# A hybrid decoder step: a new order for the seven-product MLP chunks, and one weight split per chunk on GpSimd

## The chip, the cores and the metric

One NeuronCore of one Trainium2 chip. The metric is the device time of one launch in microseconds (us). TensorE multiplies, VectorE (DVE in the rows), ScalarE (ACT) and GpSimd (POOL) do the elementwise work, SyncE (SP) and GpSimd issue the weight transfers.

## What is computed

A two-layer decoder trunk on 544 tokens (512 prompt, 8 sequences of 4), width 1024, all in float32: layer 0 mixes tokens by a gated linear recurrence, layer 1 by sliding-window attention. Behind each mixer stands the MLP that this change is about:

```python
def squared_relu_mlp(x, w_up, w_down):
    return jnp.square(jax.nn.relu(x @ w_up)) @ w_down      # 1024 -> 4096 -> 1024
x = layer_norm(ALPHA * x + squared_relu_mlp(x, mlp_w_up[i], mlp_w_down[i]), ln2_g[i], ln2_b[i])
```

## The kernel before

**Splits.** Every float32 operand is written as two parts: `hi`, the value rounded by ScalarE (a Copy into an fp32r tile), and `lo`, the rest, `raw - hi`, subtracted by VectorE. A product is three matmuls: hi·hi, lo·hi, hi·lo. A weight block or slab (128 x 1024) lies in one of 4 `stage` buffers when it arrives and in one of 8 slots of `w_hi` and `w_lo` when it is split. `s_whi` counts roundings, `s_wlo` rests.

**Chunks.** The hidden width 4096 goes in 8 chunks of 512. Chunks 0 and 7 are multiplied directly. Chunks 1 to 6 (`CHUNKS - 2` = 6) use a 2 x 2 scheme with seven products in place of eight for the up matrix and seven for the down matrix: U11, UT1, UT2, U21, UT3, UT4, U22, then D11, DT1, DT2, D22, DT3, D21, DT4. TensorE's `chunk` runs them in that order; each is 24 matmuls of 256 or 288 columns. Chunk 1 and chunk 6 are written out, 2 to 5 are one hardware loop.

**Weights.** The T blocks are sums of corner blocks. GpSimd makes them by transfers that add onto the raw block already in `stage` (`added`, L2055), in four chains per chunk, one for each stage buffer: U11, UT1, UT2, UT4; U22, UT3, D22, DT3; U21, D21; D11, DT1, DT2, DT4. Each link needs the rest of the block before it in its buffer, since the sum overwrites the raw data. SyncE loads the plain blocks (`bring`, L673) in the order of `load_around`, GpSimd issues the sums in the order of `all_sums`; both queues wait in order. In chunk 1 two blocks have a buffer of their own, `first_raw`.

**Slots.** `PLACE` gives each block its slot, `BEFORE` the block whose product must be done before that slot is overwritten (`slot_free`), 0 in this chunk, -1 in the one before. ScalarE's `split_in` (L808) waits for the raw block and for the slot, VectorE's `split_in` (L1315) for the rounding, TensorE's products for the rest (`split_done`). `split` (L802, L1309) does the same for the slabs of chunks 0 and 7.

**Around the products.** ScalarE's `keep` (L1041) copies a product's bank to SBUF before the next product accumulates over it: UT2 waits for the copy of U11's tiles (kept (0, t)), UT3 for UT2's (2, t), UT4 for UT3's (4, t). VectorE's `combine` (L1696) adds a bank onto a copy; `rectify` (L1046), `square_hi` (L1057) and `square_raw` (L1061) are the Relu and the squares. VectorE sums squares into S1 to S4 (`part_sum`, L1708), ScalarE rounds them (`part_hi`, L1066), VectorE takes their rests (`part_lo`, L1704), and the down products use them. VectorE's `settle` (L1719) adds a pair of output banks into `acc`; the numbers (j, p) of `settle` are down product and pair. The first products of chunk 7 wait for the banks of (5, 0) and (5, 1). `token_sum` (L1036) and `token_lo` (L1356) make the summed tokens once per MLP, partly within chunk 1.

Each engine's `chunk` function is its program for a chunk, a fixed order written by hand. An instruction whose wait isn't met holds everything behind it on its engine. Tables such as `KEEP_ORDER`, `SETTLE_ORDER`, `ROUND_WEIGHT` (roundings) and `REST_WEIGHT` (rests) turn the place in that order into semaphore counts.

## Time and profile before

| | |
|---|---|
| device time, median of 3 runs | 1124.59 us (1120.53 to 1125.94) |
| the profiled execution | 1123.91 us, its span 1121.7 us |
| TensorE matmul busy | 95% of the span |
| VectorE, ScalarE, GpSimd busy | 75%, 59%, 20% |
| mean granted TensorE clock | 0.973 |
| read from HBM | 135.95 MB |

The six seven-product chunks of layer 0 lie between 220 and 502 us of the span, those of layer 1 between 770 and 1054 us. A row of a timeline gives the start, the duration, the engine, the line and the operation; merged neighbours carry their number (x2), and the bracket gives the idle time before and what ended it. Neighbouring instructions of an engine overlap by about 0.1 us, so that one split of 128 x 1024 takes 1.06 us of ScalarE alone and 0.96 in a row of them.

### The profile page before, as it was taken

The page shows a single profiled execution, that of the slowest core. Times are in us where ns is not written, and L with a number is a line of the kernel's source. Part 1 is how long each engine was busy: PE and PEld are TensorE (multiplying, and loading weights), DVE is VectorE, ACT ScalarE, POOL GpSimd, SP SyncE. Part 2 cuts the span into 40 slices and gives each one's busy share as a digit, 9 for nine tenths or more (in the row PEclk, how much of TensorE's full clock was granted, in tenths as well). Part 3 has the DMA queues.
Part 4 walks back from the last instruction along what each step waited for, and adds up shares of the span by engine and source line. Part 5 has one row for each costly group of instructions (what it writes and reads, how often), then busy time and mean ns, then how long its engine had stood idle before and what let it go on. Part 6 is the DMA issues. An engine that isn't in the chain of part 4 may idle for free.

```text
span 1121.7 us, 21627 instructions
## 1 busy us (share of the span) xinstructions
PE 1067.0 (95%) x8247; PEld 1040.7 (93%) x8247; DVE 845.0 (75%) x1289; ACT 665.9 (59%) x1159; POOL 226.4 (20%) x285
## 2 busy tenths in 40 slices
PE   8999999989999999899999999998999999998996
PEld 8999999989999899899999778998999899898995
DVE  6999898868778777586875664896868678585775
ACT  5999857554654636453667775665654636445343
POOL 1111042011111111111244463200111111111023
PEclk9999999989999999998999999999999999998998
DMA  7322406176787686773141220262787686866502
GB/s 241 114 86 94 132 18 190 39 151 141 163 200 150 137 180 137 184 203 123 28 124 44 76 58 20 76 151 59 167 189 150 134 183 151 175 143 132 150 1 80
DMA packets 54460, 139.54 MB, mean 124 GB/s; under 512 B 5632, under 2 KB 21440, under 8 KB 54368
## 3 DMA queue, kind: packets, MB, share of 16 engines
q0 software_dynamic: 14512, 53.60, 27.4%
q1 hardware_dynamic: 39584, 84.32, 22.8%
q8 instruction: 50, 0.82, 0.3%
q10 hardware_dynamic: 288, 0.59, 0.2%
q14 instruction: 26, 0.21, 0.1%
HBM read 135.95 MB, written 3.56 MB: 124 GB/s over the span
## 4 chain that ended last, share of the span: by engine, by line
PE 57%; DMA 17%; DVE 12%; issue 6%; ACT 6%; POOL 2%; DVEq 0%; SPq 0%; ACTq 0%; POOLq 0%
DMA stage<-w_up 10%; PE bank L2167 8%; PE bank L2168 7%; PE bank L2169 7%; DMA stage<-w_down 7%; DVE w_lo L1315 5%; PE bank L2422 3%; PE bank L2424 3%; PE bank L2423 3%; PE bank L2254 3%; PE bank L2443 3%; PE bank L2441 3%; PE bank L2442 3%; PE bank L2255 3%; PE bank L2256 3%
## 5 line engine op out<-in xcount | busy, mean ns | idle before, releaser
L808 ACT ACTIVATE w_hi<-stage 128x1024 fp32r<-128x1024 f32 x164 | 170.5, 1055 | 246.7 <-DMA stage<-w_up 117.1
L1315 DVE TENSOR_TENSOR w_lo<-stage,w_hi 128x1024 fp32r<-128x1024 f32 x164 | 194.8, 1219 | 78.0 <-ACT w_hi L808 77.8
L2441 PE MATMUL bank<-part_hi,w_hi 128*128 128x288 f32 (+1 forms) x672 | 194.9, 290 | 0.4 <-DVE part_lo L1704 0.3
L2443 PE MATMUL bank<-part_hi,w_lo 128*128 128x288 f32 (+1 forms) x672 | 194.8, 290 | 0.0
L2442 PE MATMUL bank<-part_lo,w_hi 128*128 128x288 f32 (+1 forms) x672 | 194.4, 289 | 0.0
L2167 PE MATMUL bank<-x_hi,w_hi 128*128 128x288 f32 (+1 forms) x496 | 145.2, 293 | 1.0 <-issue 1.0
L2168 PE MATMUL bank<-x_lo,w_hi 128*128 128x288 f32 (+1 forms) x496 | 143.7, 290 | 0.0
L2169 PE MATMUL bank<-x_hi,w_lo 128*128 128x288 f32 (+1 forms) x496 | 143.1, 288 | 0.0
L2441 PEld LDWEIGHTS bank<-part_hi,w_hi 128*128 128x128 f32 x672 | 127.2, 189 | 0.8 <-issue 0.5
L2442 PEld LDWEIGHTS bank<-part_lo,w_hi 128*128 128x128 f32 x672 | 127.5, 190 | 0.0
L2443 PEld LDWEIGHTS bank<-part_hi,w_lo 128*128 128x128 f32 x672 | 127.3, 189 | 0.0
L2422 PE MATMUL bank<-s_hi,w_hi 128*128 128x288 f32 (+1 forms) x384 | 114.5, 298 | 9.4 <-ACT h L1041 9.3
L1719 DVE TENSOR_TENSOR acc<-acc,bank 128x512 f32<-128x512 f32 (+1 forms) x168 | 113.0, 709 | 8.9 <-PE bank L2443 8.8
L2423 PE MATMUL bank<-s_lo,w_hi 128*128 128x288 f32 (+1 forms) x384 | 112.9, 294 | 0.0
L2424 PE MATMUL bank<-s_hi,w_lo 128*128 128x288 f32 (+1 forms) x384 | 112.7, 294 | 0.0
L2422 PE MATMUL bank<-x_hi,w_hi 128*128 128x256 f32 (+1 forms) x288 | 89.5, 311 | 22.8 <-ACT h L1041 19.0
L2055 POOL DMA_DIRECT2D stage<-w_down x48 | 41.4, 863 | 267.7 <-DVE w_lo L1315 267.7
L2167 PEld LDWEIGHTS bank<-x_hi,w_hi 128*128 128x128 f32 x496 | 93.2, 188 | 2.3 <-issue 2.1
L2169 PEld LDWEIGHTS bank<-x_hi,w_lo 128*128 128x128 f32 x496 | 93.4, 188 | 0.0
L2168 PEld LDWEIGHTS bank<-x_lo,w_hi 128*128 128x128 f32 x496 | 93.3, 188 | 0.0
L2055 POOL DMA_DIRECT2D stage<-w_up x44 | 41.7, 949 | 253.5 <-DVE w_lo L1315 231.6
L2254 PE MATMUL bank<-x_hi,w_hi 128*128 128x256 f32 (+1 forms) x288 | 85.0, 295 | 5.3 <-DVE acc L1719 5.3
(293 smaller groups left out, 2954.8 us busy)
## 6 DMA issues: line engine op xcount, KB each, us to landing
stage<-w_up SPq DMA_DIRECT2D x54, 512.0 KB, 3.9
stage<-w_down SPq DMA_DIRECT2D x52, 512.0 KB, 5.8
stage<-w_down POOLq DMA_DIRECT2D x48, 512.0 KB, 5.5
stage<-w_up POOLq DMA_DIRECT2D x44, 512.0 KB, 7.4
stage<-w_qkv SPq DMA_DIRECT2D x10, 512.0 KB, 4.3
stage<-w_x SPq DMA_DIRECT2D x8, 512.0 KB, 5.0
stage<-w_y SPq DMA_DIRECT2D x8, 512.0 KB, 3.4
stage<-w_out SPq DMA_DIRECT2D x8, 512.0 KB, 3.7
```

The costliest lines, as they stand in the source:

```text
L808: A(w_hi[:, slot_of(l, k), :], raw_of(l, c, k), ACT.Copy).then_inc(s_whi, 1)
L1315: vt.tensor_tensor(w_lo[:, s, :], raw_of(l, c, k), w_hi[:, s, :].bitcast(F32), ALU.subtract)\
L2167: mm(out, wh, xh, start=(k == 0), stop=False)
L2168: mm(out, wh, xl, start=False, stop=False)
L2169: ins = mm(out, wl, xh, start=False, stop=(k == last))
L2254: mm(out, wh, xh, start=(k == 0), stop=False)
L2422: mm(out, wh, xh[:, k, :], start=(fresh and k == 0), stop=False, skip_group_check=True)
L2423: mm(out, wh, xl[:, k, :], start=False, stop=False, skip_group_check=True)
L2424: ins = mm(out, wl, xh[:, k, :], start=False, stop=(k == 3), skip_group_check=True)
L2441: mm(out, wh, xh[:, k, :], start=(fresh and k == 0), stop=False, skip_group_check=True)
L2442: mm(out, wh, xl[:, k, :], start=False, stop=False, skip_group_check=True)
L2443: ins = mm(out, wl, xh[:, k, :], start=False, stop=(k == 1), skip_group_check=True)
```

## The change

- The order of work on ScalarE, VectorE, SyncE and GpSimd within a chunk is new, with new tables; TensorE's order is not touched. UT1 of the next chunk is rounded before S4 and DT4 and its rest taken before the settlings from (2, 1) on; D11's load is issued behind U22's and its rounding behind the copy (0, 0); the squares of H11 move behind the copies of UT3's tiles; settling (5, 1) comes before (5, 0).
- New slots: UT1 has one of its own, UT2 shares with UT4 and DT3, D11 with D21, U21 with D22, DT1 with DT4, U22 with DT2.
- The rest of D21 is taken by GpSimd (`side_rest`), counted by a semaphore of its own, `s_side`; VectorE's last rest of a chunk, DT4, counts two on `s_wlo`.
- GpSimd issues UT1's sum of the next chunk before DT4's, and UT2's and UT3's at the end of its chunk.
- Before chunk 1, U22 is split before UT2, and UT3's sum is issued right behind it.
- The four up slabs of chunk 7 are loaded and split within chunk 6, where the blocks of a next chunk would have been (`bring_slab`, `slab_in`). In layer 0 the cache transfers on GpSimd's queue wait until chunk 7's slabs are split.

The diff, with the parts that only repeat one of these left out:

```diff
-REST_ORDER = (H11, H22, S1, S2, H12, S4, S3)
+REST_ORDER = (H11, H22, S1, H12, S2, S4, S3)
...
-PLACE = {U11: 0, UT3: 0, U22: 1, UT1: 2, UT4: 2, DT2: 2, UT2: 3,
-         D11: 4, DT3: 4, DT1: 5, D21: 5, U21: 6, D22: 6, DT4: 6}
+PLACE = {U11: 0, UT3: 0, UT1: 1, U22: 2, DT2: 2, UT2: 3, UT4: 3, DT3: 3, U21: 4, D22: 4,
+         D11: 5, D21: 5, DT1: 6, DT4: 6}
...
-FIRST = (U11, UT1, UT2, U22)
+FIRST = (U11, UT1, U22, UT2)
...
-KEEP_ORDER = ((0, 0), (0, 1), (2, 1), (2, 0), (4, 0), (4, 1), (5, 1))
+KEEP_ORDER = ((0, 0), (0, 1), (2, 0), (2, 1), (4, 0), (4, 1), (5, 1))
...
         def split_done(l, c, k, i=0):
 
+            if k == D21:
+                return s_side, i + (before(l, c) + 1)
             return s_wlo, i * SPLITS + (rest_at[(l, c, k)] + 1)
...
             def load_around(l, c, i=0):
 
                 last = c == CHUNKS - 2
-                if c > 1:
-                    bring(l, c, D11, s_xd, down_block(l, c, 0, 0, i), split_done(l, c - 1, DT4, i))
                 bring(l, c, D22, s_yin, down_block(l, c, 1, 1, i), split_done(l, c, UT3, i))
                 if not last:
                     bring(l, c + 1, U11, s_xu, up_block(l, c + 1, 0, 0, i), split_done(l, c, UT1 if c == 1 else UT4, i))
+                else:
+                    bring_slab(l, 0)
                 bring(l, c, D21, s_zin, down_block(l, c, 1, 0, i), split_done(l, c, U21, i))
                 if not last:
                     bring(l, c + 1, U22, s_yin, up_block(l, c + 1, 1, 1, i), split_done(l, c, DT3, i))
+                else:
+                    bring_slab(l, 1)
+                    bring_slab(l, 3)
+                    bring_slab(l, 2)
+                if not last:
+                    bring(l, c + 1, D11, s_xd, down_block(l, c + 1, 0, 0, i), split_done(l, c, DT4, i))
                 if not last:
                     bring(l, c + 1, U21, s_zin, up_block(l, c + 1, 1, 0, i), split_done(l, c, D21, i))
```

In ScalarE's `chunk`:

```diff
+                keep(l, c, i, 0, 0, 4, h11[:, 0, 0:256])
                 split_in(l, c, D11, i)
-                keep(l, c, i, 0, 0, 4, h11[:, 0, 0:256])
                 split_in(l, c, U21, i)
...
                 split_in(l, c, UT4, i)
-                keep(l, c, i, 2, 1, 4, h12[:, 1, :], -1.0)
...
                 keep(l, c, i, 2, 0, 4, h12[:, 0, :], -1.0)
+                keep(l, c, i, 2, 1, 4, h12[:, 1, :], -1.0)
                 split_in(l, c, DT1, i)
                 rectify(l, c, i, H11, h_low)
+                split_in(l, c, D22, i)
+                keep(l, c, i, 4, 0, 4, h22[:, 0, :], -1.0)
                 square_hi(l, H11, h_low)
-                square_raw(h_low)
-                keep(l, c, i, 4, 0, 4, h22[:, 0, :], -1.0)
-                split_in(l, c, D22, i)
                 keep(l, c, i, 4, 1, 4, h22[:, 1, :], -1.0)
...
                 part_hi(l, c, i, S2)
+                split_in(l, c, DT3, i)
                 split_in(l, c, D21, i)
+                if not last:
+                    split_in(l, c + 1, UT1, i)
+                else:
+                    slab_in(l, 1)
                 part_hi(l, c, i, S4)
-                split_in(l, c, DT3, i)
                 split_in(l, c, DT4, i)
...
                 if not last:
                     split_in(l, c + 1, U22, i)
+                else:
+                    slab_in(l, 2)
                 if not last:
                     split_in(l, c + 1, UT2, i)
+                else:
+                    slab_in(l, 3)
```

In VectorE's `chunk`:

```diff
                 part_lo(l, c, i, S1)
-                settle(l, c, i, 0, 0)
+                split_in(l, c, DT2, i)
                 dve.wait_ge(*summed(l, c, S1, i))
                 dve.wait_ge(*squared(l, c, H11, i))
                 part_sum(h22[:, :, :], h22[:, :, :], h11[:, :, :], ALU.subtract)
-                split_in(l, c, DT2, i)
+                settle(l, c, i, 0, 0)
+                part_lo(l, c, i, H12)
                 part_lo(l, c, i, S2)
-                part_lo(l, c, i, H12)
+                settle(l, c, i, 0, 1)
                 dve.wait_ge(*summed(l, c, S2, i))
                 part_sum(h12[:, :, :], h12[:, :, :], h22[:, :, 0:256], ALU.add)
-                settle(l, c, i, 0, 1)
+                settle(l, c, i, 1, 1)
                 settle(l, c, i, 1, 0)
                 part_lo(l, c, i, S4)
+                part_lo(l, c, i, S3)
+                split_in(l, c, DT3, i)
                 settle(l, c, i, 2, 0)
-                settle(l, c, i, 1, 1)
-                split_in(l, c, DT3, i)
-                part_lo(l, c, i, S3)
+                if not last:
+                    split_in(l, c + 1, UT1, i)
+                else:
+                    slab_in(l, 1)
                 settle(l, c, i, 2, 1)
                 settle(l, c, i, 3, 0)
                 settle(l, c, i, 3, 1)
-                split_in(l, c, D21, i)
-                if not last:
-                    split_in(l, c + 1, UT1, i)
                 split_in(l, c, DT4, i)
...
+                settle(l, c, i, 5, 1)
                 settle(l, c, i, 5, 0)
                 settle(l, c, i, 6, 0)
-                settle(l, c, i, 6, 1)
-                slabs(2)
-                settle(l, c, i, 5, 1)
                 if not last:
                     split_in(l, c + 1, UT2, i)
-                slabs(3)
+                else:
+                    slab_in(l, 3)
+                settle(l, c, i, 6, 1)
```

In VectorE's `mlp`, before chunk 1, and on GpSimd:

```diff
                 split_in(l, 1, U11)
                 split_in(l, 1, UT1)
+                split_in(l, 1, U22)
                 accumulate_pair(l, 1, 0)
+                split_in(l, 1, UT2)
                 accumulate_pair(l, 1, 2)
                 accumulate_pair(l, 1, 4)
                 accumulate(l, 6)
                 accumulate(l, 7)
-                split_in(l, 1, UT2)
-                split_in(l, 1, U22)
                 token_sum_4(l)
-                token_lo(l, 3, s4_lo[:, :, :], s4_hi[:, :, :], raw_b[:, :, 0:256])
                 chunk(l, 1)
...
+            def side_rest(l, c):
+
+                s = slot_of(l, D21)
+                pool.wait_ge(s_whi, round_at[(l, c, D21)] + 1)
+                pt.tensor_tensor(w_lo[:, s, :], raw_of(l, c, D21), w_hi[:, s, :].bitcast(F32), ALU.subtract)\
+                    .then_inc(s_side, 1)
...
+                up_sum(l, 1, UT3, 0, 1, s_uy, split_done(l, 1, U22))
                 for c in range(1, CHUNKS - 1):
-                    if c > 1:
-                        up_sum(l, c, UT2, 1, 1, s_ux, split_done(l, c, UT1))
-                    up_sum(l, c, UT3, 0, 1, s_uy, split_done(l, c, U22))
                     up_sum(l, c, UT4, 1, 0, s_first if c == 1 else s_ux, split_done(l, c, UT2))
                     down_sum(l, c, DT1, 0, 1, s_dx, split_done(l, c, D11))
                     down_sum(l, c, DT2, 1, 1, s_dx, split_done(l, c, DT1))
                     down_sum(l, c, DT3, 0, 1, s_dy, split_done(l, c, D22))
-                    down_sum(l, c, DT4, 1, 0, s_dx, split_done(l, c, DT2))
                     if c < CHUNKS - 2:
                         up_sum(l, c + 1, UT1, 0, 1, s_ux, split_done(l, c + 1, U11))
+                    down_sum(l, c, DT4, 1, 0, s_dx, split_done(l, c, DT2))
+                    side_rest(l, c)
+                    if c < CHUNKS - 2:
+                        up_sum(l, c + 1, UT2, 1, 1, s_ux, split_done(l, c + 1, UT1))
+                    if c < CHUNKS - 2:
+                        up_sum(l, c + 1, UT3, 0, 1, s_uy, split_done(l, c + 1, U22))
```

## Rows read from the trace of the kernel before

**Rows 1.** The page's first part: engine busy time, share of the span, instructions.

```profile
PE 1067.0 (95%) x8247; PEld 1040.7 (93%) x8247; DVE 845.0 (75%) x1289; ACT 665.9 (59%) x1159; POOL 226.4 (20%) x285
```

**Rows 2.** TensorE's waits over the whole run: line <- who ended it: us, times, longest.

```profile
PE bank L2422 <- ACT h L1041: 28.4, 19, 3.6
...
PE bank L2254 <- DVE acc L1719: 5.3, 3, 2.0
...
PE bank L2422 <- DVE w_lo L1315: 3.8, 2, 2.3
```

**Rows 3.** The twelve chunks as windows; after POOL: TensorE clock, DMA share, GB/s.

```profile
220.09:271.74 51.65, 47.06 (x338) 46.47 (x337) 39.43 (x46) 26.30 (x36) 7.82 (x9) 0.90 0.64 135
...
317.33:360.75 43.42, 43.11 (x338) 42.80 (x337) 34.70 (x42) 24.86 (x35) 6.96 (x8) 1.00 0.77 168
...
406.67:453.96 47.29, 44.73 (x338) 44.29 (x337) 34.52 (x42) 24.58 (x35) 6.96 (x8) 0.96 0.71 157
...
sum 566.10, PE 533.54 PEld 527.82 DVE 419.86 ACT 299.13 POOL 82.81; mean PE 44.46 PEld 43.99 DVE 34.99 ACT 24.93 POOL 6.90
```

**Rows 4.** TensorE's timeline in chunk 5 of layer 0; start, duration, instruction, [idle before].

```profile
406.69 0.28 PE L2422 MATMUL bank<-x_hi,w_hi 128*128 128x256 f32 x1
...
424.92 0.40 PE L2422 MATMUL bank<-x_hi,w_hi 128*128 128x288 f32 x1 [2.30 <-ACT h L1041]
...
441.84 0.28 PE L2441 MATMUL bank<-part_hi,w_hi 128*128 128x256 f32 x1
...
453.97 0.28 PE L2422 MATMUL bank<-x_hi,w_hi 128*128 128x256 f32 x1
```

**Rows 5.** Windows behind the longer waits; the clock stands after POOL.

```profile
503.90:510.80 6.90, 4.88 (x24) 4.68 (x23) 5.67 (x6) 2.11 (x2) 0.00 (x0) 0.54 0.64 196
...
425.40:428.80 3.40, 3.40 (x18) 3.40 (x17) 2.65 (x3) 2.92 (x5) 0.47 (x1) 0.58 0.85 133
...
1022.80:1029.60 6.80, 5.66 (x24) 5.69 (x25) 2.83 (x4) 3.61 (x7) 1.72 (x2) 0.53 0.62 87
```

**Rows 6.** ScalarE's timeline in chunk 5 of layer 0.

```profile
409.48 2.01 ACT L808 ACTIVATE w_hi<-stage 128x1024 fp32r<-128x1024 f32 x2 [8.11 <-DMA stage<-w_up]
...
421.81 1.06 ACT L808 ACTIVATE w_hi<-stage 128x1024 fp32r<-128x1024 f32 x1 [2.70 <-DMA stage<-w_down]
...
436.21 0.69 ACT L1066 ACTIVATE part_hi<-h 128x576 fp32r<-128x576 f32 x1 [0.21 <-DVE h L1708]
```

**Rows 7.** The chain that ended last, chunk 5 of layer 0.

```profile
401.37 8.09 DMA stage<-w_up
...
413.23 8.48 DMA stage<-w_down
```

**Rows 8.** VectorE's timeline in chunk 5 of layer 0.

```profile
434.16 0.75 DVE L1704 TENSOR_TENSOR part_lo<-h,part_hi 128x576 fp32r<-128x576 f32 x1
...
437.23 1.35 DVE L1704 TENSOR_TENSOR part_lo<-h,part_hi 128x576 fp32r<-128x576 f32 x2
...
446.01 3.49 DVE L1315 TENSOR_TENSOR w_lo<-stage,w_hi 128x1024 fp32r<-128x1024 f32 x3
```

**Rows 9.** Instruction groups of GpSimd, the same split in attention.

```profile
L2128 POOL TENSOR_TENSOR w_lo<-stage,w_hi 128x1024 fp32r<-128x1024 f32 x8 | 19.1, 2384 | 12.5 <-ACT w_hi L802 12.4
```

**Rows 10.** Timelines of VectorE (DVE) and GpSimd (POOL) around 145 us.

```profile
144.98 0.42 DVE L1574 TENSOR_TENSOR sum_a<-acc,sum_a 128x256 f32<-128x256 f32 x1
145.32 0.42 DVE L1562 TENSOR_TENSOR acc<-bank,acc 128x256 f32<-128x256 f32 x1
145.77 1.35 DVE L1574 TENSOR_TENSOR sum_a<-acc,sum_a 128x256 f32<-128x256 f32 x1
145.41 1.43 POOL L2012 TENSOR_TENSOR m_lo<-z,m_hi 128x576 fp32r<-128x576 f32 x1 [1.62 <-ACT m_hi L872]
```

**Rows 11.** The issuing line of GpSimd's transfers.

```profile
DMA to landing us min/median/max: 5.2/6.1/11.9
```

**Rows 12.** GpSimd's timeline in chunk 5 of layer 0.

```profile
438.14 1.22 POOL L2055 DMA_DIRECT2D stage<-w_up  x1
```

More of the change, by code:

```diff
@@ L440, in plan_mlp_jobs @@
             for c in range(1, CHUNKS - 1):
-                here = [ahead for _, ahead in ROUND_WEIGHT if c + ahead < CHUNKS - 1]
                 for table, at in ((ROUND_WEIGHT, round_at), (REST_WEIGHT, rest_at)):
-                    ours = [(c + ahead, w) for w, ahead in table if c + ahead < CHUNKS - 1]
-                    for k, (cw, w) in enumerate(ours):
-                        at[(l, cw, w)] = start + k
-                start += len(here)
+                    for k, (w, ahead) in enumerate(table):
+                        end = c + ahead == CHUNKS - 1
+                        at[(l, c + ahead, SLAB_AFTER.index(w) if end else w)] = start + k
+                start += SPLITS
             while len(jobs) < start:
@@ L449, in plan_mlp_jobs @@
                 jobs.append(None)
-            for n, k in enumerate((UT4, DT3, D21, DT4)):
-                last_on[(st0 + n) % STAGES] = rest_at[(l, CHUNKS - 2, k)]
-            ring[0] = w0 + 8 * (CHUNKS - 1)
-            plan_jobs(("chunk", l, CHUNKS - 1), "w" * 8)
+            for n in (0, 0, 0, 1):
+                loads[(st0 + n) % STAGES] += 16
+                up_slab_at[l].append(((st0 + n) % STAGES, loads[(st0 + n) % STAGES]))
+            w7 = w0 + 8 * (CHUNKS - 1)
+            job_at[("chunk", l, CHUNKS - 1)] = (start - 4, w7)
+            after = (None, rest_at[(l, CHUNKS - 2, DT4)],
+                     rest_at[(l, CHUNKS - 1, 2)], rest_at[(l, CHUNKS - 1, 3)])
+            for k, n in enumerate((2, 3, 0, 1)):
+                st = (st0 + n) % STAGES
+                loads[st] += 16
+                emptied[len(jobs)] = after[k]
+                where.append((st, loads[st]))
+                last_on[st] = len(jobs)
+                jobs.append(("w", w7 + 4 + k))
+            ring[0] = w7 + 8
+            turn[0] += 2
         def split_done(l, c, k, i=0):
+            if k == D21:
+                return s_side, i + (before(l, c) + 1)
             return s_wlo, i * SPLITS + (rest_at[(l, c, k)] + 1)
@@ L705, in load_mlp @@
                 load_around(l, CHUNKS - 2)
-                for k in range(4):
-                    load(j7 + k, up_quad(l, CHUNKS - 1, k))
+                sp.wait_ge(*split_done(l, CHUNKS - 2, D21))
                 for k in range(4):
@@ L1154, in mlp @@
                 chunk(l, CHUNKS - 2)
-                split(range(j7, j7 + 4))
                 for q in range(4):
@@ L1315, in split_in, with slab_in @@
                 vt.tensor_tensor(w_lo[:, s, :], raw_of(l, c, k), w_hi[:, s, :].bitcast(F32), ALU.subtract)\
+                    .then_inc(s_wlo, 2 if k == DT4 else 1)
+            def slab_in(l, k):
+                st, s = up_slab_at[l][k][0], (job_at[("chunk", l, CHUNKS - 1)][1] + k) % SLOTS
+                dve.wait_ge(s_whi, round_at[(l, CHUNKS - 1, k)] + 1)
+                vt.tensor_tensor(w_lo[:, s, :], stage[:, st, :], w_hi[:, s, :].bitcast(F32), ALU.subtract)\
                     .then_inc(s_wlo, 1)
@@ L1720, in settle, with chunk @@
                     .then_inc(s_acc, 1)
-            def chunk(l, c, i=0, slabs=lambda k: None):
+            def chunk(l, c, i=0):
                 first, last = c == 1, c == CHUNKS - 2
                 split_in(l, c, D11, i)
+                if first:
+                    token_lo(l, 3, s4_lo[:, :, :], s4_hi[:, :, :], raw_b[:, :, 0:256])
                 split_in(l, c, U21, i)
@@ L1737, in chunk @@
                     split_in(l, c + 1, U11, i)
+                else:
+                    slab_in(l, 0)
+                part_lo(l, c, i, H11)
                 part_lo(l, c, i, H22)
@@ L1765, in chunk @@
                 settle(l, c, i, 3, 1)
-                split_in(l, c, D21, i)
-                if not last:
-                    split_in(l, c + 1, UT1, i)
                 split_in(l, c, DT4, i)
@@ L1829, in mlp @@
                     chunk(l, 2, i)
-                chunk(l, CHUNKS - 2, slabs=lambda k: split([j7 + k]))
+                chunk(l, CHUNKS - 2)
                 for q in range(4):
```

55 lines of the change are left out of this document (35 added, 20 removed).

## The prediction, made before the changed kernel ran

> **What bounds the kernel now.** I started with the busy shares. TensorE computes in 1067.0 of 1121.7 us and no other engine passes 75% [rows 1]: the kernel is TensorE's instruction stream plus what interrupts it. The waits of that engine say where it is interrupted: 28.4 us behind ScalarE's copies of product tiles out of the banks (L1041), 3.8 us behind weight rests on VectorE (L1315), 5.3 us behind VectorE's additions into `acc` (L1719) [rows 2]. The first two groups lie in the six seven-product chunks of each MLP, the third at the start of the chunk behind them. Cut by chunk, the twelve take 43.4 to 51.7 us each, 566.1 us in all [rows 3].
>
> What would a chunk take without waits? In chunk 5 of layer 0 its last four products (256, 288, 256 and 288 columns, 24 matmuls each, 26,112 columns) run from 441.84 to 453.97, 12.13 us [rows 4]. A chunk has 92,160 columns, so 42.8 us; the one chunk that hardly waited took 43.42 [rows 3]. Twelve make 513.7, so **52.4 us** are lost in the chunks. About 32 of them are idle (28.4 + 3.8); most of the rest is the clock. Behind the longer waits the granted clock falls to its lower level (1.2 of 2.4 GHz): 0.58 on average in 425.4 to 428.8, right behind a 2.30 us wait [rows 4, 5]. 3.4 us at half clock cost 1.7.
>
> Why does it wait? Follow chunk 5, which starts at 406.69. UT4's product starts only at 424.92, after 2.30 us idle for a copy of UT3's tile [rows 4]. In ScalarE's fixed order that copy stands behind DT1's split, made at 421.81, a Relu and two squares [rows 6]. DT1's split waited for an accumulating transfer of 8.48 us, in flight from 413.23 on, when D11's rest was ready [rows 7]. D11 was split right behind UT2 at 409.48 [rows 6], and UT2 waited for its own 8.09 us transfer [rows 7]. UT2's transfer needed UT1's rest, which stands on VectorE behind D21's at the end of the chunk before; for the chunk after this one it is the second of the three at 446.01, ready at 448.3 [rows 8]. This loop through two transfers closes once per chunk.
>
> **The change, part by part.** TensorE's program keeps its products and their order, so nothing comes off its work; what can go is waiting. A block of the next chunk is written with a prime, a time within a chunk as +t from its start.
>
> *UT1' earlier.* D21's rest leaves VectorE and UT1's moves ahead of three settlings. The pair at 437.23 gives 0.67 for a rest of 576 columns, the three at 446.01 give 1.15 for a weight's; a settling and a 512-column rest take 0.6 by their width [rows 8]. S1's rest starts at 434.16; behind it the new queue is DT2's split 1.15, sum S2 0.67, a settling 0.6, rests of H12 0.6 and S2 0.67: it ends at 438.5. DT2's product starts at 441.84 less its own 3.2, 438.65 [rows 4]. Then settling 0.6, sum S4 0.6, two settlings 1.2, rest of S4 0.65: 441.6 to 441.7, against D22's product at 441.84. Both fit by 0.1. Behind them rest S3 0.7, DT3 1.15, settling 0.6, UT1' 1.15: 445.3 in place of 448.3.
>
> *GpSimd's split.* Its price is on the trace: the same instruction in attention takes 2384 ns [rows 9], twice VectorE's. GpSimd's queue has room, 6.96 us busy in a 47.29 us chunk [rows 3]. The hidden part is what it does to VectorE. At 145.41 GpSimd runs a 1.43 us subtract; VectorE's add of two SBUF tiles, 0.42 at 144.98, takes 1.35 at 145.77 and ends 0.28 behind GpSimd's [rows 10], while the add at 145.32, which reads a bank, keeps its 0.42. So an SBUF-SBUF operation of VectorE stands until GpSimd's ends. The Trainium skill says it as a rule (SBUF — State Buffer, "SBUF: two separate sides": one exclusive lock for the whole instruction, the loser blocks); by that rule, the trace agrees. D21's rounding ends on ScalarE at 439.5: S2's copy (436.21 before, now 0.6 later, ends 437.5) [rows 6], then DT3 and D21, 1.0 each (two splits take 2.01 at 409.48). GpSimd then holds from about 439.7 to 442.1. VectorE's settlings read banks and pass; S4's rest, due at 441.05, ends at 442.8 where D22's product wanted it at 441.84. **New wait: 1.0 us per chunk** (bounds: 0 if GpSimd falls into a gap, 2.4 if all of it stands in the way: 45.6 per chunk, 547.2, and the sum below would be 1095 in place of 1078). All behind it shifts by that too: UT1' ready 446.3.
>
> *UT2' and D11'.* GpSimd's queue in front of UT2' is DT4's issue (ready by 437) and the split (done 442.1), so UT2' goes out at 446.5, 2.1 earlier. With the 8.1 of before [rows 7] it is in by 454.8, with the fastest transfer's 5.2 [rows 11] by 451.7, against a next chunk start of 455.0. ScalarE now copies tile (0, 0) first, possible 1.6 after the start, so D11' is split at +1.9 in place of +3.75 (409.48 plus 1.0, less 406.69). UT1' has a slot of its own, DT4 needs DT1's slot instead of D22's, UT4 needs UT2's product (+9.2): none ends last. UT3' goes out behind U22' and is wanted at about +4. On SyncE's queue D11's load moves behind U22's, whose wait (DT3's rest) ends earlier than D11's own (DT4's rest): no delay; with the 8.1 us of a shared transfer it lands at about +2, when ScalarE comes to it.
>
> *DT1 and the copies.* D11's rounding (1.0), rest (1.15) and the issue (0.3) put DT1's transfer at +4.4; it takes 8.48 (UT4's and D22's beside it as before). DT1's split +13.0 to +14.0; Relu 0.6; the split of D22 0.96 in place of two squares 1.15; copy (4, 0) at +15.5, done +15.85 where the product wants it at +15.3 to 15.5. **Remaining wait 0.4** (0 to 1.9). Tile (2, 0) is now copied before (2, 1), in the order the products want them. UT1' is accumulated before DT4, beside DT3: issued some 8 us earlier than the 438.14 of before [rows 12], wanted at 439.4.
>
> *First chunks.* Their 51.65 and 49.7 come from UT3 (transfer issued behind UT2, U22 and five additions) and from S4's rest in front of D11's. U22 before the additions and UT3's transfer right behind it move it some 7 us; S4's rest stands behind D11. I cost them like the others.
>
> *Last slabs.* Four slab loads enter the gaps of chunk 6 in place of loads that chunk didn't have; they accumulate nothing. The last chunk's first products use the banks of settlings (5, 0), (5, 1); (5, 1) stood last, behind three slab rests. The 5.3 us idle [rows 2] and, in layer 0, 6.9 us at 0.54 clock [rows 5], 3.4 lost, half of it taken for layer 1 whose wait was shorter, make 10.4; I take 9.8. The hidden cache transfers of layer 0, held until the slabs are in, have over 100 us before attention reads them: nothing.
>
> **Sum.** 42.8 + 1.0 + 0.4 = 44.2 per chunk, 530.4 for twelve, 35.7 less; 9.8 at the ends. The profiled execution took 1123.91 (span 1121.7), the median is 1124.59: 1123.9 - 35.7 - 9.8 = **1078.4**.
>
> **Rivals.** *GpSimd finds a gap* (0.2): D21 is rounded a little earlier or later and its subtract runs beside bank-reading settlings. 43.1 per chunk, 517.2: 1123.9 - 48.9 - 9.8 = 1065. For it: the settlings in that stretch; against: by the rows D21's rounding ends 1.5 us before S4's rest is due, and GpSimd needs 2.4.
>
> *The transfers stay late* (0.21): more of them run at once around the chunk's start (UT2', UT3', D11', U21'), and DT1 or D22 lands 1.5 us later than I take. 42.8 + 1.0 + 1.9 = 45.7, 548.4: 1096.4. For it: the same transfer takes 5.2 to 11.9 [rows 11]; against: UT2' has 1 to 4 us to spare. The full 2.4 us block would come out at the same place (1095) and shares this chance.
>
> *S4 stands behind UT1'* (0.06; the slower side): on ScalarE S4's rounding now comes behind UT1's split, which waits for a transfer. Issued beside DT3's and taking the longest 11.9 [rows 11] it lands 31.5 after the start; D22's product waits some 3.2 us. After the longest stall of before, 3.6 us, the clock was low for 6.8 us (0.53) [rows 2, 5]: 3.4 more. 42.8 + 0.4 + 3.2 + 3.4 = 49.8, 597.6: 1123.9 + 31.5 - 9.8 = 1145.6. It decides from 48.0 per chunk on. Against it: pairs issued like that took under 9 us in the steady chunks.
>
> *Little comes of it* (0.03): within half a per cent, if half of the last one happens.
>
> **The numbers.** 0.5 for the forecast with 1071 to 1087 of its own. The range takes in both neighbours and the floor without any wait (1123.9 - 52.4 - 10.4 = 1061): 1061 to 1104; above it lies the slower rival and part of the third. A measurement here tells about 0.5% (5.6 us) from no change. Faster 0.91, same 0.03, slower 0.06.
>
> **What would show it.** Right: chunk windows of 43.5 to 45 us; TensorE's waits for L1041 from 28.4 to under 8; a new wait of TensorE for VectorE's rests (part_lo), some 12 us in 12 times; clock 1.00 in most chunks; GpSimd's split at 2.4 us with a VectorE operation beside it that takes over 1.5. Wrong: waits for UT4's copy that stay at 2 us, or part_lo waits over 2 us with low clock behind them.

## The result and the profile after

| | before | after |
|---|---|---|
| device time, median | 1122.86 us (4 runs) | 1073.74 us (4 runs, 1071.94 to 1075.26) |
| ratio, 95% interval | | 0.956 (0.953 to 0.959) |
| the profiled execution, its span | 1123.91, 1121.7 us | 1074.01, 1072.0 us |
| twelve seven-product chunks | 566.1 us | 525.8 us |
| everything outside them | 555.6 us | 546.2 us |
| mean granted TensorE clock | 0.973 | 0.994 |

Forecast 1078.4, measured 1073.7. The busy shares and the clock by slices come first on the page of the changed kernel:

```profile
PE 1047.3 (98%) x8247; PEld 1021.7 (95%) x8247; DVE 839.7 (78%) x1277; ACT 662.2 (62%) x1159; POOL 257.3 (24%) x297
...
PEclk9999999999999999999999999999999999999998
```

Against [rows 1], TensorE does the same 8247 matmuls in 19.7 us less, so that much was clock and not idle time; of the 49.7 us of span the rest, 30.0, was idle time. GpSimd has 31 us more, twelve splits. TensorE's waits, in the columns of [rows 2]:

```profile
PE bank L2504 <- DVE part_lo L1752: 4.7, 8, 0.6
PE bank L2300 <- DVE w_lo L1350: 3.8, 2, 2.2
PE bank L2504 <- issue: 2.4, 4, 0.6
```

The 28.4 us behind `keep` and the 5.3 behind `settle` are gone (their lines are now L1077 and L1767), and so are the 3.8 behind weight rests within the chunks. The second line is not new: it lies outside the chunks and stood at 3.4 us before. What is new is the first line and the third: D22's product waits 0.6 us for the rest of S4, in each of the twelve chunks (8 + 4 times; "issue" means only that the profile names no releaser). The chunks, in the columns of [rows 3]: the first two and the last of layer 0, and the sum of all twelve:

```profile
220.47:264.02 43.55, 42.95 (x338) 42.74 (x337) 38.16 (x45) 26.68 (x37) 8.70 (x8) 1.00 0.73 162
264.02:307.98 43.96, 43.37 (x338) 42.80 (x337) 34.09 (x42) 24.58 (x35) 9.57 (x9) 1.00 0.78 171
...
439.83:483.38 43.55, 42.93 (x338) 42.73 (x337) 33.02 (x41) 26.26 (x37) 6.96 (x6) 1.00 0.71 168
...
sum 525.81, PE 518.66 PEld 513.28 DVE 415.22 ACT 301.85 POOL 107.71; mean PE 43.22 PEld 42.77 DVE 34.60 ACT 25.15 POOL 8.98
```

The chunks before differed by 8 us among themselves; these are alike to 0.02 within a kind (43.55 for the first and the last, 43.95 for the four of the loop). I read this as a sign that no chunk waits for a transfer any more: GpSimd's transfers still take anything from 5.2 to 12.9 us from issue to landing, and a chunk that waited for one would show it (below, with UT1' late again, the chunks do differ). Matmul busy plus idle is 43.37 + 0.59 in a chunk of the loop. The place is in the timelines of chunk 5, of TensorE, VectorE and GpSimd:

```profile
426.73 0.29 PE L2506 MATMUL bank<-part_hi,w_lo 128*128 128x288 f32 x1
427.61 0.38 PE L2504 MATMUL bank<-part_hi,w_hi 128*128 128x256 f32 x1 [0.59 <-DVE part_lo L1752]
...
422.00 1.36 DVE L1752 TENSOR_TENSOR part_lo<-h,part_hi 128x512 fp32r<-128x512 f32 x2
...
424.47 1.41 DVE L1767 TENSOR_TENSOR acc<-acc,bank 128x576 f32<-128x576 f32 x2
425.80 2.25 DVE L1752 TENSOR_TENSOR part_lo<-h,part_hi 128x512 fp32r<-128x512 f32 x2
427.97 1.21 DVE L1356 TENSOR_TENSOR w_lo<-stage,w_hi 128x1024 fp32r<-128x1024 f32 x1
...
424.18 2.65 POOL L2123 TENSOR_TENSOR w_lo<-stage,w_hi 128x1024 fp32r<-128x1024 f32 x1 [2.21 <-ACT w_hi L836]
```

The two rests of 512 columns at 425.80 take 2.25 where the same pair at 422.00 takes 1.36: the first of them, S4's, stands until GpSimd's subtract ends at 426.83. The chain of waits gives its own duration:

```profile
425.80 1.59 DVE part_lo L1752
```

1.59 in place of 0.69. The two settlings at 424.47, which read a bank and lie wholly beside GpSimd's subtract, take 1.41, as always. D22's product starts 0.88 behind the matmul before it, where 0.13 is usual.

### The profile page after: what moved, and what is told of

The parts are those of the page before. It is cut to its first block, busy times and chain, and to the rows that moved or that the text cites. A ratio compares the mean times of both kernels' runs of the same rounds, so it can differ in the third digit from the quotient of the medians.

```text
span 1072.0 us, 21616 instructions
## 1 busy us (share of the span) xinstructions
PE 1047.3 (98%) x8247; PEld 1021.7 (95%) x8247; DVE 839.7 (78%) x1277; ACT 662.2 (62%) x1159; POOL 257.3 (24%) x297
## 3 DMA queue, kind: packets, MB, share of 16 engines
q1 hardware_dynamic: 39584, 84.32, 23.5%
## 4 chain that ended last, share of the span: by engine, by line
PE 86%; DVE 8%; issue 3%; ACT 1%; DMA 1%; POOL 0%; DVEq 0%; SPq 0%; ACTq 0%
PE bank L2485 8%; PE bank L2230 8%; PE bank L2487 8%; PE bank L2486 8%; PE bank L2231 8%; PE bank L2232 8%; PE bank L2504 6%; PE bank L2506 6%; PE bank L2505 6%; PE bank L2317 3%; PE bank L2318 3%; PE bank L2319 3%; DVE part_lo L1752 2%; DVE h L1756 2%; DVE acc L1767 2%
## 5 line engine op out<-in xcount | busy, mean ns | idle before, releaser
L836 ACT ACTIVATE w_hi<-stage 128x1024 fp32r<-128x1024 f32 x164 | 168.0, 1053 | 137.9 <-DMA stage<-w_up 80.7
L1356 DVE TENSOR_TENSOR w_lo<-stage,w_hi 128x1024 fp32r<-128x1024 f32 x152 | 182.0, 1217 | 58.9 <-ACT w_hi L836 58.8
L1767 DVE TENSOR_TENSOR acc<-acc,bank 128x512 f32<-128x512 f32 (+1 forms) x168 | 113.9, 707 | 8.2 <-PE bank L2506 8.2
L2485 PE MATMUL bank<-x_hi,w_hi 128*128 128x256 f32 (+1 forms) x288 | 83.1, 289 | 0.0
L2317 PE MATMUL bank<-x_hi,w_hi 128*128 128x256 f32 (+1 forms) x288 | 82.8, 287 | 0.0
L2318 PE MATMUL bank<-x_lo,w_hi 128*128 128x256 f32 (+1 forms) x288 | 82.5, 287 | 0.0
```

What stands on the lines that cost most here:

```text
L836: A(w_hi[:, slot_of(l, k), :], raw_of(l, c, k), ACT.Copy).then_inc(s_whi, 1)
L1356: vt.tensor_tensor(w_lo[:, s, :], raw_of(l, c, k), w_hi[:, s, :].bitcast(F32), ALU.subtract)\
L1767: vt.tensor_tensor(a, a, bank[:, b0:b0 + 2, 0:n], ALU.subtract if j in (2, 4) else ALU.add)\
L2485: mm(out, wh, xh[:, k, :], start=(fresh and k == 0), stop=False, skip_group_check=True)
```

## The experiments

Each is the changed kernel with one edit, unless it says otherwise. Ratios are to the kernel before, measured beside it.

| kernel | time, us | ratio (95%) |
|---|---|---|
| changed kernel | 1073.7 | 0.956 (0.953 to 0.959) |
| D21's rest on VectorE | 1063.5 | 0.946 (0.943 to 0.949) |
| GpSimd's split placed beside settlings | 1063.8 | 0.947 (0.943 to 0.950) |
| before, with GpSimd's split alone | 1109.3 | 0.987 (0.983 to 0.991) |
| before, with UT1' ahead of D21 on VectorE | 1107.5 | 0.989 (0.985 to 0.992) |
| UT1' at its old place | 1086.7 | 0.968 (0.964 to 0.972) |
| work before chunk 1 in the old order | 1081.3 | 0.962 (0.958 to 0.967) |
| ScalarE's old order at two copies | 1074.0 | 0.958 (0.955 to 0.961) |
| last slabs late | 1073.2 | 0.956 (0.952 to 0.959) |
| settling (5, 1) last | 1077.2 | 0.960 (0.956 to 0.963) |
| both of these | 1079.1 | 0.962 (0.957 to 0.967) |
| D21 on VectorE, TensorE's loop written out | 1062.2 | 0.946 (0.943 to 0.950) |
| the same, ScalarE's and VectorE's too | 1058.9 | 0.944 (0.940 to 0.949) |

**Is the new wait GpSimd's doing?** First D21's rest back on VectorE, between two settlings:

```diff
                 settle(l, c, i, 3, 0)
+                split_in(l, c, D21, i)
                 settle(l, c, i, 3, 1)
...
-                    side_rest(l, c)
```

> The changed kernel with one part undone: D21's rest is taken by VectorE again, between the settlings (3, 0) and (3, 1); GpSimd does no split, everything else is as changed. Theory (the SBUF-to-SBUF rest of S4 waits until GpSimd's subtract ends, and that is the 0.8 us wait in front of D22's product in every chunk): with GpSimd's subtract gone that wait goes, and D21's rest (1.15 us) finds room in VectorE's queue before D21's product wants it. Chunks of 43.1 to 43.3 us in place of 43.95, so 8 to 10 us less than the changed kernel: about 1064 us, ratio to the kernel before 0.947. Rival (VectorE has no room, and the change needs GpSimd): S4's rest is late anyway and D21's product now waits too: 44.5 us per chunk or more, 1080 us, ratio 0.962.

Measured 1063.5. A chunk of the loop and the one behind it, as windows:

```profile
390.19:433.29 43.10, 43.10 (x338) 42.76 (x337) 34.15 (x43) 24.48 (x35) 6.91 (x8) 1.00 0.80 170
433.29:476.00 42.71, 42.71 (x338) 42.71 (x337) 33.83 (x43) 26.00 (x37) 4.32 (x5) 1.00 0.74 175
```

Matmul busy equals the window: no idle time at all. VectorE's extra 1.2 us per chunk costs nothing and 10.2 us come off. Giving work to the idle engine was a loss.

**Or only its moment?** GpSimd keeps the split but waits for DT3's rest with it, and UT1' goes behind three settlings, so that these lie beside it:

```diff
+                pool.wait_ge(*split_done(l, c, DT3))
                 pool.wait_ge(s_whi, round_at[(l, c, D21)] + 1)
```

> The changed kernel with GpSimd's split of D21 held until VectorE has taken DT3's rest, and UT1' moved on VectorE behind the settlings (2, 1), (3, 0), (3, 1), so that GpSimd's 2.4 us run beside operations that read a bank. Theory (blocking of SBUF-to-SBUF operations only, and 3.7 us of slack for UT1'): the 0.8 us wait in front of D22's product goes and nothing takes its place: 43.1 to 43.3 us per chunk, 1064 us, ratio 0.947, and GpSimd's subtract takes 2.4 us in place of 2.65. Rival (settlings are held by GpSimd too): DT3's product waits about 1 us for the settling of DT2's second pair instead: 44 us per chunk, 1074 us, ratio 0.956. Second rival (UT1' has no slack): the copy of UT3's tiles comes late again, waits of 1 us or more in front of UT4's product.

Measured 1063.8, the chunks as above (43.10 and 42.71). VectorE and GpSimd in chunk 5:

```profile
421.21 1.22 DVE L1356 TENSOR_TENSOR w_lo<-stage,w_hi 128x1024 fp32r<-128x1024 f32 x1
422.34 2.48 DVE L1767 TENSOR_TENSOR acc<-acc,bank 128x512 f32<-128x512 f32 x4
...
422.51 2.40 POOL L2124 TENSOR_TENSOR w_lo<-stage,w_hi 128x1024 fp32r<-128x1024 f32 x1 [6.40 <-DVE w_lo L1356]
```

Four settlings in 2.48, 0.62 each, beside the whole of the subtract, and the subtract at 2.40 against 2.65 in the changed kernel. So what cost 10 us was not GpSimd's slower subtract but what lay beside it. The Trainium skill's rule (SBUF — State Buffer, "SBUF: two separate sides"), one exclusive lock held for the whole instruction with the loser blocked, agrees: 1.59 for the rest beside it, 0.62 for each settling. That the split stands beside settlings is as good as not having it on GpSimd, and no better: VectorE has room for it.

**What made the old loop slow?** The kernel before with GpSimd's split as its only change:

```diff
                 settle(l, c, i, 3, 1)
-                split_in(l, c, D21, i)
                 if not last:
                     split_in(l, c + 1, UT1, i)
```

> The kernel before with this part of the change alone: D21's rest on GpSimd, behind UT1's sum in its queue; UT1' and DT4 move up on VectorE by the freed 1.15 us. Theory (the loop through UT1', UT2's transfer, D11' and DT1's transfer sets the chunk's length; GpSimd's subtract blocks S4's rest, but TensorE has 0.6 us in hand there): the loop gets shorter by about 1 us where GpSimd doesn't block more than that: 1112 to 1123 us, ratio 0.99 to 1.00. Rival (GpSimd's part brings the gain): 1100 us or less, ratio below 0.98. Other rival (blocking dominates): slower, 1128 to 1140 us, ratio 1.005 to 1.015.

Measured 1109.3, a bigger gain than the theory expected (1112 to 1123) and a smaller one than the rival (1100 or less); it lies between the two. Without the split, D21's rest still on VectorE but behind UT1's:

```diff
-                split_in(l, c, D21, i)
                 if not last:
                     split_in(l, c + 1, UT1, i)
+                split_in(l, c, D21, i)
                 split_in(l, c, DT4, i)
```

> The kernel before with one thing changed: on VectorE the rest of UT1' stands ahead of the rest of D21 instead of behind it. GpSimd takes no split. Theory (the old loop ran from D21's rest through UT1' to the last transfers, and any 1.15 us taken out of it brings the stalls under the size at which the clock fell): chunks of 44 to 45.5 us, the granted clock near 1.00 in all of them, and the ratio of the kernel with GpSimd's split alone or a little better, 0.980 to 0.988. Rival (that kernel gained because VectorE had less work, and an order of the same work gives nothing): the long stalls stay, ratio 0.996 to 1.002.

Measured 1107.5; 0.989 stands just outside the 0.980 to 0.988, and far from the rival's 0.996. Two of its chunks of the loop, the second and the fifth of layer 0, and its largest wait:

```profile
272.56:317.69 45.13, 43.05 (x338) 42.75 (x337) 34.78 (x42) 25.51 (x36) 6.96 (x8) 1.00 0.76 166
406.99:451.97 44.98, 43.22 (x338) 42.76 (x337) 34.62 (x42) 24.95 (x35) 6.96 (x8) 1.00 0.75 163
...
PE bank L2441 <- DVE w_lo L1315: 15.4, 10, 2.1
```

Chunks 2 to 6 of both layers sum to 464.7 us before, 446.7 with GpSimd's split alone, 444.2 with the two rests exchanged, 438.7 in the changed kernel and 427.1 in the last experiment. So most of the steady gain is UT1' being ready one rest earlier, by either way, and the chunk hits a next wait in both: here D21's product, whose rest is now behind UT1's; with GpSimd's split alone D22's product, for the old placement puts a rest beside GpSimd again. VectorE and GpSimd of that kernel, chunk 5:

```profile
435.09 2.47 DVE L1709 TENSOR_TENSOR part_lo<-h,part_hi 128x512 fp32r<-128x512 f32 x1
...
434.62 2.39 POOL L2075 TENSOR_TENSOR w_lo<-stage,w_hi 128x1024 fp32r<-128x1024 f32 x1 [0.71 <-ACT w_hi L813]
```

0.69 becomes 2.47, and here GpSimd is not slowed. The gain is more than the 1.15 us of a rest: 1.8 to 2.1 per chunk. In these ten chunks TensorE's idle time falls from 23.5 us to 13.8 with GpSimd's split alone and to 13.4 with the two rests exchanged, and the same matmuls take 441.2, 432.9 and 430.8 us. So about half is stalls and half is the low clock behind them: the clock reads 0.93 to 0.96 in five of the ten chunks before and 1.00 in all ten of either kernel. The converse, in the changed kernel: UT1' rounded and rested behind DT4, so that it is the second rest behind the settlings again:

```diff
                 split_in(l, c, D21, i)
-                if not last:
-                    split_in(l, c + 1, UT1, i)
                 part_hi(l, c, i, S4)
                 split_in(l, c, DT4, i)
+                if not last:
+                    split_in(l, c + 1, UT1, i)
```

> The changed kernel with UT1' back where it stood: on ScalarE behind S4 and DT4, on VectorE behind the settlings (3, 0), (3, 1) and DT4's rest; slots, copies and GpSimd's split as changed. Theory (the loop through UT1', UT2', D11' and DT1 set the length before, and moving UT1' is what opened it): UT1's rest comes 4 us later than in the changed kernel, UT2' is split about 1 to 3 us behind the next chunk's start in place of 3.1 us ahead of it, D11' 0.4 to 2.3 us later, and the wait for the copy of UT3's tiles comes back: 44.3 to 46 us per chunk, 1077 to 1094 us, ratio 0.959 to 0.974. Rival (the slots and the copies' order opened it): 43.95 us per chunk as in the changed kernel, 1074 us, ratio 0.956.

Measured 1086.7, 13 us more. Its wait, and ScalarE in chunk 5 (which starts at 399.31) with the product that waits:

```profile
PE bank L2485 <- ACT h L1077: 7.7, 12, 1.3
...
400.81 1.06 ACT L836 ACTIVATE w_hi<-stage 128x1024 fp32r<-128x1024 f32 x1 [7.29 <-DMA stage<-w_up]
...
412.02 1.06 ACT L836 ACTIVATE w_hi<-stage 128x1024 fp32r<-128x1024 f32 x1 [1.23 <-DMA stage<-w_down]
...
414.75 0.39 ACT L1077 ACTIVATE h<-bank 128x288 f32<-128x288 f32 x1
...
415.20 0.40 PE L2485 MATMUL bank<-x_hi,w_hi 128*128 128x288 f32 x1 [0.46 <-ACT h L1077]
```

The loop of the kernel before is back link by link: UT2's split waits for its transfer until 1.5 us into the chunk, DT1's split for its own, and UT4's product for the copy of (4, 0) behind that. The chunks of the loop differ again, 44.4 to 46.1 us. Even in the new order the steady chunks depend on UT1' being early.

**The first chunks.** The order of roundings and rests before chunk 1 put back (UT2, then U22, behind the additions):

```diff
-FIRST = (U11, UT1, U22, UT2)
+FIRST = (U11, UT1, UT2, U22)
...
-                split_in(l, 1, U22)
                 accumulate_pair(l, 1, 0)
-                split_in(l, 1, UT2)
...
                 accumulate(l, 7)
+                split_in(l, 1, UT2)
+                split_in(l, 1, U22)
```

> The changed kernel with the part before chunk 1 undone: UT2 is split before U22, and both behind the five additions on VectorE, as in the kernel before; GpSimd's sum of UT3 still waits for U22's rest and so goes out 5 us later. The order within chunk 1 stays as changed. Theory (the first chunks' 51.65 and 49.71 us came from UT3's late arrival, with a low clock behind the stall): both first chunks get 3 to 6 us longer than their 43.6, 1080 to 1085 us, ratio 0.962 to 0.967, and no other chunk changes. Rival (it came from S4's token rest in front of D11's): less than 1 us per first chunk, ratio 0.957.

Measured 1081.3. Chunk 1 takes 47.17 and 47.69 us in the two layers in place of 43.55, the others are unchanged. That gives back 7.7 of the 14.3 us that the two first chunks gained (101.4 to 87.1). The wait that returns stands within UT2's product (3.1 us, for a copy by ScalarE); the other of before, 1.57 us idle in front of U21's product for a weight's rest, does not. What took that one away no run took apart.

**ScalarE's order.** D11's split ahead of the copy of (0, 0), and the squares of H11 ahead of that of (4, 0), as before:

```diff
+                split_in(l, c, D11, i)
                 keep(l, c, i, 0, 0, 4, h11[:, 0, 0:256])
-                split_in(l, c, D11, i)
...
                 rectify(l, c, i, H11, h_low)
-                split_in(l, c, D22, i)
-                keep(l, c, i, 4, 0, 4, h22[:, 0, :], -1.0)
                 square_hi(l, H11, h_low)
+                square_raw(h_low)
+                keep(l, c, i, 4, 0, 4, h22[:, 0, :], -1.0)
+                split_in(l, c, D22, i)
```

> The changed kernel with ScalarE's old order around the two copies: the split of D11 ahead of the copy of (0,0) again, and the squares of H11 ahead of the copy of (4,0), D22's split behind it. Theory (both copies have slack now, since UT2's split is in some 3 us before the next chunk starts and the copy of (4,0) stands at 14.9 us of a chunk): no wait comes back at UT4's product or at UT1's, the time is within 1.5 us of the changed kernel, ratio 0.955 to 0.957. Rival (the order on ScalarE is what took the last 0.3 to 0.4 us per chunk at UT4's product away, as the prediction had it for its copy): that wait returns with 0.3 us or more per chunk in 12 chunks, 1078 us or more, ratio 0.960 or more.

Measured 1074.0, no difference; the kernel's ratio of 0.958 lies above the 0.957, its time within the 1.5 us. ScalarE's copy of (4, 0) and the product that overwrites its bank, in chunk 5 of this kernel:

```profile
409.68 0.39 ACT L1077 ACTIVATE h<-bank 128x288 f32<-128x288 f32 x1
...
410.13 0.40 PE L2485 MATMUL bank<-x_hi,w_hi 128*128 128x288 f32 x1
```

It ends at 410.07, 0.06 ahead. Now that the transfers are early, ScalarE gets there in time in either order.

**The end of a layer's MLP.** Three kernels: the slabs of chunk 7 loaded and split behind chunk 6 as before; (5, 1) last; both, with the third slab's rest ahead of (5, 1) as before.

```diff
-                settle(l, c, i, 5, 1)
                 settle(l, c, i, 5, 0)
                 settle(l, c, i, 6, 0)
                 if not last:
                     split_in(l, c + 1, UT2, i)
                 settle(l, c, i, 6, 1)
+                if last:
+                    slab_in(l, 2)
+                settle(l, c, i, 5, 1)
```

> The changed kernel with the last slabs undone: chunk 7's four up slabs are loaded one into each stage buffer as these empty, rounded behind chunk 6 on ScalarE, their rests taken where the kernel before took them; the order of the settlings and the held cache transfers stay as changed. Theory (the waits at chunk 7's start came from settling (5, 1), which stood last, and from a slab that came late beside the cache transfers): with both cured, the early slabs are worth little: at most 2 us more than the changed kernel, ratio 0.956 to 0.958. Rival (the early slabs bring it): 5 to 10 us more, ratio 0.960 to 0.965.

> The changed kernel with settling (5, 1) behind (5, 0), (6, 0) and (6, 1) again, in every chunk. Theory: chunk 7's third and fourth tile wait for it until 1.4 us behind chunk 6's end, 1.2 us per layer, 2 to 3 us more than the changed kernel in all: 1076 to 1077 us, ratio 0.958 to 0.959; inside the chunks nothing changes. Rival (nothing waits for it there): 1074 us, ratio 0.956.

> The changed kernel with both ends of a layer's MLP undone together: the slabs of chunk 7 loaded and split behind chunk 6, and settling (5, 1) last, behind the rest of the third of those slabs, as before. Theory (the 9.4 us that the kernel gained outside the twelve chunks are one wait, a settling behind slab splits, and either of the two edits shortens it; each alone was worth 0 and 3.4 us): the third product of chunk 7 waits some 2 us in each layer and the clock falls behind it, 5 to 9.5 us over the changed kernel, 1079 to 1083.5 us, ratio 0.960 to 0.966. Rival (the two effects add, and the rest of the gain came from elsewhere): 1077 us, the same as with the settling alone, ratio 0.959.

Measured 1073.2, 1077.2 and 1079.1. TensorE's wait for settlings in the second and in the third:

```profile
PE bank L2317 <- DVE acc L1767: 3.3, 2, 1.9
```
```profile
PE bank L2307 <- DVE acc L1758: 3.7, 2, 1.9
```

Early slabs alone bring nothing, the settling's place 3.4 us (expected were 2 to 3), and both together 5.4. The stretch behind the last chunk of layer 1 takes 67.5 us before, 63.9 in the changed kernel and 67.5 again with both undone: there the two edits are the whole gain. Between the MLPs of the two layers it is 268.0, 261.9 and 264.0, so 4.0 of 6.2 us are not theirs. Before, that stretch opened with two waits (1.45 and 2.02 us) and the low clock of [rows 5]; with both undone it has one wait, of 1.87, and in its first 10 us the clock stays at 1.00:

```profile
482.87:493.25 10.38, 8.51 (x72) 8.31 (x71) 5.29 (x6) 2.57 (x4) 0.00 (x0) 1.00 0.58 196
```

In the kernel before, VectorE stood 2.79 us for a slab's rounding just ahead of the first of the two, and the rounding stood for the slab's load:

```profile
491.32 8.85 DMA stage<-w_up
```

All three kernels leave one thing as changed: the cache transfers of layer 0 stay held until chunk 7's slabs are split. Before, GpSimd's queue issues these five transfers from 485.7 us on, and the three loads of `w_up` slabs behind them take 6.5 to 8.9 us. In layer 1, which has no such transfers, the same loads take 3.6 to 4.7 in the same kernel, although its last seven-product chunk runs late too (50.12 us), and there the end of the MLP has one wait of 1.87, exactly as with both undone. With both undone the loads of layer 0 take 3.5 to 5.5. So the 4.0 us go most likely to the held cache transfers. That is argued from traces: no run put these transfers back alone.

**The last 0.4 us of a chunk.** In the kernel with D21's rest on VectorE, chunks 2 to 5 take 43.10 and the written-out ones 42.71. TensorE's loop written out, then ScalarE's and VectorE's as well:

```diff
-                with pe.Fori(0, CHUNKS - 4) as i:
-                    chunk(l, 2, i)
+                for c in range(2, CHUNKS - 2):
+                    chunk(l, c)
```

> The changed kernel with D21's rest on VectorE (as in e1_rest_on_vector) and TensorE's loop over chunks 2 to 5 written out as four chunks, so that it has no register in its waits and no loop end; the other engines keep their loops. Theory (chunks 2 to 5 take 43.10 us in e1_rest_on_vector and chunks 1 and 6, which are written out, 42.71; the 0.39 us lie on waits that no engine was late for, so they are TensorE's own): 42.71 us in all twelve, 3 us less, 1060.4 us, ratio 0.9435. Rival (the longer program costs as much in instruction loading, or the 0.39 us belong to the chunks' heavier traffic): no difference, ratio 0.946.

> The kernel with D21's rest on VectorE and TensorE's loop over chunks 2 to 5 written out, with ScalarE's and VectorE's loops over them written out too. Theory (the 0.29 us that chunks 2 to 5 still take over chunks 1 and 6 come from the loops of the other engines, whose waits compare with a register and so are late by a little): all twelve chunks at 42.7 to 42.8, 2.3 us less, 1059.5 to 1060.5 us. Rival (they come from the traffic of a next chunk's blocks, which chunk 6 does not have, or from a copy that is late by its place): chunks 2 to 5 stay at 43.0, 1062 us, ratio 0.946.

The first brings chunks of 43.00 in place of the 42.71 expected. Its 1062.2 us (expected 1060.4) can't be told from the 1063.5 with the loop, so this reading rests on the windows: TensorE's own loop is 0.1 of the 0.39. The second brings 1058.9, a little under the expected 1059.5 to 1060.5, and a chunk of the loop and the last one read:

```profile
388.92:431.62 42.70, 42.70 (x338) 42.70 (x337) 34.14 (x43) 24.58 (x35) 6.91 (x8) 1.00 0.81 173
431.62:474.32 42.70, 42.70 (x338) 42.70 (x337) 34.14 (x43) 25.90 (x37) 4.32 (x5) 1.00 0.75 176
```

The rest were the loops of the other two engines, not the traffic, which is the same. It beats both kernels: 0.944 of the time before, 0.986 of the changed kernel's. All twelve chunks are now TensorE's instruction stream and nothing else (512.5 us).

## Why the prediction was right, and where it was off

- **The bound.** Right. The floor was taken as 42.8 from twelve microseconds of four products; measured 42.71, 1.1 us over twelve chunks.
- **The loop through UT1' and two transfers.** Right, and tested both ways: cutting 1.15 us out of it in the kernel before gains 13 to 14 us (against that kernel measured beside it), and putting it back in the changed one loses 13. UT1' was to be ready 8.7 us ahead of the next chunk's start (455.0 less 446.3); measured 439.83 less 430.91, 8.9.
- **UT2' and D11'.** UT2's issue was forecast at 8.5 us ahead of that start and stands at 8.6; it was to land 0.2 to 3.3 ahead (446.5 plus 8.1 is 454.6, so the 0.2 should be 0.4). ScalarE's timeline:

```profile
436.77 1.06 ACT L836 ACTIVATE w_hi<-stage 128x1024 fp32r<-128x1024 f32 x1 [2.72 <-DMA stage<-w_up]
```

  3.1 ahead, the short end. D11' is split at +1.9 as forecast, behind the copy of (0, 0).
- **DT1 and the copy of (4, 0).** The term that was too big. DT1's split was put at +13.0 from a transfer of 8.48 us. ScalarE, chunk 5 (start 395.87):

```profile
406.81 1.06 ACT L836 ACTIVATE w_hi<-stage 128x1024 fp32r<-128x1024 f32 x1
408.97 0.63 ACT L1082 ACTIVATE h<-h 128x512 f32<-128x512 f32 x1 [1.10 <-DVE h L1744]
409.78 1.06 ACT L836 ACTIVATE w_hi<-stage 128x1024 fp32r<-128x1024 f32 x1 [0.18 <-PE bank L2487]
410.75 0.39 ACT L1077 ACTIVATE h<-bank 128x288 f32<-128x288 f32 x1
```

  The split comes at +10.9 with no wait for a transfer (there is no bracket); then ScalarE waits for VectorE's `combine`, and the copy comes at +14.9 in place of +15.5, in time. The forecast's remaining wait of 0.4 per chunk is 0. The transfer went out at +4.5, as forecast (+4.4), but took 5.4 us in place of 8.48. Such transfers did not get faster in general, the 48 onto `w_down` have a median of 5.5 us on both pages; DT1's did, from a median of 8.3 over the twelve chunks to 5.6 (6.7 with UT1' late). The forecast had UT4's and D22's transfers beside it "as before". GpSimd issues UT4's and DT1's like this, chunk 5 before and after:

```profile
412.10 0.87 POOL L2055 DMA_DIRECT2D stage<-w_up  x1 [6.26 <-DVE w_lo L1315]
413.23 0.87 POOL L2055 DMA_DIRECT2D stage<-w_down  x1 [0.27 <-DVE w_lo L1315]
...
396.67 0.86 POOL L2107 DMA_DIRECT2D stage<-w_up  x1 [3.15 <-DVE w_lo L1356]
400.38 0.87 POOL L2107 DMA_DIRECT2D stage<-w_down  x1 [2.85 <-DVE w_lo L1356]
```

  1.1 us apart before, 3.7 now, with D22's load 2.2 behind in both. That this spacing is what made DT1's transfer shorter is a reading of the traces, which no run isolates.

- **GpSimd's split.** The mechanism was right and its size near: 1.0 per chunk forecast, 0.85 measured in the chunks of the loop (43.95 against 43.10 with the rest on VectorE: 0.75 until D22's product starts, 0.10 in its first matmuls) and 0.84 in the others (43.55 against 42.71), 10.2 in all; idle time alone is 7.1 us in 12 waits, where some 12 were foretold. The price taken was 2.4; it took 2.65 here, since it began while VectorE's sum S4, an SBUF-SBUF operation, was still running. The rival by which GpSimd finds a gap would have had 1065; the two experiments that make that gap give 1063.5 and 1063.8.
- **The slower rival.** S4 behind UT1' on ScalarE did not come: its rounding starts at 424.95, 0.8 us ahead of VectorE's turn for it, since UT1's transfer was in.
- **First chunks.** Costed like the others, and they are even 0.4 shorter, for they stand outside the loops. Right in size; the order before chunk 1 is half of it.
- **The ends.** 9.8 forecast, 9.4 measured (6.2 behind layer 0's chunks and 3.6 behind layer 1's, less a start that is 0.4 later). Right as a sum, since it was read off the waits and the low clock as a whole, whatever caused them. The reasons given, the settling's place and the slabs, hold for all of layer 1 and for 2.1 us of layer 0. The prediction put the held cache transfers at "nothing", having asked only whether attention would miss them and not what they did to the slab loads beside them; as argued above, the other 4.0 us are most likely theirs.
- **A cost not foreseen.** The hardware loops: 0.39 us in each of eight chunks. The 43.42 us chunk of [rows 3] lies in the loop, and the prediction read its 0.6 above the floor as "hardly waited".

The sum of the misses in the chunks: 530.4 less 525.8 is 4.6. Of these 1.1 is the floor and 1.8 GpSimd's wait (12.0 forecast, 10.2 measured). The last 1.7 are the remaining wait (4.8 forecast, nothing measured) less the loops (nothing forecast, 3.1 measured). That these two largely make up for each other is luck: 44.2 per chunk came near the 43.95 of the loop with one term that was not there in place of one that was overlooked. The profiled execution took 1074.0, 4.4 less than forecast: 4.6 in the chunks and 0.2 outside the span (2.2 before, 2.0 after), with the ends making up 0.4 the other way.

## What to carry to other kernels

Where each step of a loop waits for a transfer that itself waits for a step before, look for the one link that stands behind unrelated work, and move it forward before taking work away: an exchange of two rests in the old kernel was worth as much as giving one to another engine. Work handed to GpSimd was free here only beside operations of VectorE that read a bank; ahead of that, ask whether VectorE was the bound at all, for here it had room and the best kernels keep the rest on it. When chunks become equal to the hundredth, look for what is left in a fixed order or in the loop itself, and no longer in the transfers. And before a term is put at nothing, ask what else it runs beside: a transfer that nobody waits for can make another one late.

## What the runs showed that was not expected

- A hardware loop costs on engines that are not the bound. With no idle time recorded on TensorE, chunks in loops took 43.10 us and written-out ones 42.71; writing out TensorE's loop took away 0.10, ScalarE's and VectorE's the other 0.29. It shows as slightly longer spacings at the products that wait for their work, not as a wait in any view.
- Who pays in a collision depends on who was first. GpSimd's subtract took 2.39 where it started first and the VectorE rest beside it 2.47 (0.69 alone); it took 2.65 where a VectorE sum was already running, and the rest behind that sum 1.59.
- Taking one rest of 1.15 us out of the old loop gained 1.8 to 2.1 us per chunk: about 1.0 of idle time, and as much again because the clock (0.96 in the fifth chunk of [rows 3]) read 1.00 in every steady chunk.
- The five cache transfers, which nobody waited for, stood beside loads of 512 KB that took 6.5 to 8.9 us; without them such loads took 3.5 to 5.5.
